# Seven products of quarters for the memory queries and a convolution input, and sums of x in two steps

## What is computed

```python
proj = x @ w_in                                        # (576, 1024) @ (1024, 8192)
cb, cc, ch, rq, rk, rv, rg, mq, gl = split(proj)       # mq: memory queries, 4 x 128 columns; cc: 4 x 128
conv_y = short_conv(cc * ch, ...)                      # cc is the convolution's second input
mk, mv = mem @ w_mem_kv                                # memory keys and values, just before mq
...
hdn = square(relu(x @ w_up))                           # four groups g of 1024 columns
x = layer_norm(alpha * x + hdn @ w_down)
```

## Time and profile before

| | us |
|---|---|
| median of 3 runs | 2177.59 |
| lowest, highest | 2177.37, 2181.48 |
| the profiled execution: its own time | 2177.93 |
| the profiled execution: its span | 2176.1 |
| TensorE busy in that span | 2133.9 |
| GpSimd busy | 1324.7 |
| VectorE busy | 1083.9 |
| ScalarE busy | 508.9 |

### The profile page before, as it was taken

The page is one execution under the profiler, slowest core; times in us unless marked ns, Lnnn a source line. Parts: engine busy times, 40 slices in busy tenths (PEclk is TensorE's granted clock), DMA queues, the critical chain, the costliest instruction groups (busy, mean ns, idle before and its releaser), DMA issues.

```text
span 2176.1 us, 39024 instructions
## 1 busy us (share of the span) xinstructions
PE 2133.9 (98%) x16116; PEld 2088.5 (96%) x16116; DVE 1083.9 (50%) x1713; ACT 508.9 (23%) x909; POOL 1324.7 (61%) x1545
## 2 busy tenths in 40 slices
PE   8999999999999999999999999999999999999997
PEld 8998999999998999999999989999999989999997
DVE  7156300533278863525791572006424798625257
ACT  3121011041013242414141210210410231414132
POOL 6644557645684938375866446676456758475574
PEclk9999999999999999999999999999999999999999
DMA  5324424234221323222324143332342213122321
GB/s 184 112 58 160 128 81 136 73 107 165 83 97 59 97 74 102 78 78 79 96 63 123 59 158 114 114 119 69 115 166 89 87 59 97 60 96 78 98 88 54
DMA packets 199928, 215.23 MB, mean 99 GB/s; under 512 B 5216, under 2 KB 192608, under 8 KB 199776
## 3 DMA queue, kind: packets, MB, share of 16 engines
q1 hardware_dynamic: 170304, 172.84, 25.5%
q10 hardware_dynamic: 29472, 40.20, 5.5%
HBM read 199.06 MB, written 13.97 MB: 98 GB/s over the span
## 4 chain that ended last, share of the span: by engine, by line
PE 91%; DVE 8%; ACT 1%; issue 0%; DMA 0%; ACTq 0%; DVEq 0%
PE gp L524 50%; PE gp L1038 12%; PE gp L540 7%; PE gp L550 7%; PE qb L630 6%; PE gp L693 4%; PE gp L867 1%; PE gp L879 1%; PE qb L661 1%; PE gp L688 1%; DVE r L2048 1%; DVE x_sum L2065 1%; DVE r L1939 1%; DVE dacc L1895 0%; DVE qb L1936 0%; DVE sqacc L1924 0%
## 5 line engine op out<-in xcount | busy, mean ns | idle before, releaser
L439 POOL TENSOR_TENSOR w_lo<-stage,w_hi 128x256 fp32r<-128x256 f32 x1072 | 870.8, 843 | 52.5 <-ACT w_hi L1250 30.0
L436 POOL TENSOR_SCALAR w_hi<-stage 128x1024 fp32r<-128x1024 f32 (+1 forms) x268 | 287.4, 1073 | 567.4 <-PE gp L524 258.1
L524 PE MATMUL gp<-b_hi,w_hi 128*128 128x288 f32 x1408 | 305.9, 299 | 7.0 <-DVE r L2060 7.0
L524 PE MATMUL gp<-x_hi,w_hi 128*128 128x288 f32 x1408 | 304.0, 298 | 0.0
L524 PE MATMUL gp<-b_hi,w_lo 128*128 128x288 f32 x1408 | 302.5, 297 | 0.0
L524 PE MATMUL gp<-b_lo,w_hi 128*128 128x288 f32 x1408 | 302.3, 296 | 0.0
L524 PE MATMUL gp<-x_lo,w_hi 128*128 128x288 f32 x1408 | 301.2, 295 | 0.0
L524 PE MATMUL gp<-x_hi,w_lo 128*128 128x288 f32 x1408 | 301.1, 295 | 0.0
L524 PEld LDWEIGHTS gp<-b_hi,w_hi 128*128 128x128 f32 x1408 | 228.1, 190 | 11.3 <-issue 11.0
L524 PEld LDWEIGHTS gp<-x_hi,w_hi 128*128 128x128 f32 x1408 | 226.9, 189 | 2.9 <-issue 2.6
L524 PEld LDWEIGHTS gp<-b_hi,w_lo 128*128 128x128 f32 x1408 | 227.9, 190 | 0.0
(11 more groups left out here) (275 smaller groups left out, 4371.5 us busy)
## 6 DMA issues: line engine op xcount, KB each, us to landing
stage<-in_w_in SPq DMA_DIRECT2D x62, 1024.0 KB, 5.8
stage<-in_w_up SPq DMA_DIRECT2D x32, 1024.0 KB, 5.4
stage<-in_w_down SPq DMA_DIRECT2D x32, 1024.0 KB, 5.0
stage<-in_w_ret_out SPq DMA_DIRECT2D x8, 1024.0 KB, 5.3
stage<-in_w_mem_kv SPq DMA_DIRECT2D x8, 1024.0 KB, 4.9
stage<-in_w_out SPq DMA_DIRECT2D x8, 1024.0 KB, 4.9
s_in_c<-in_ret_state ACTq DMA_DIRECT2D x8, 512.0 KB, 4.6
out_ret_sample<-s_in_c ACTq DMA_DIRECT2D x8, 512.0 KB, 3.4
```

Of the source, the lines that this page charges most:

```text
L436: nc.gpsimd.tensor_scalar(hi, raw, 1.0, 1.0, ALU.mult, ALU.mult).then_inc(hi_done, 1)
L439: ins = nc.gpsimd.tensor_tensor(lo[:, k:k + 2, :], raw[:, k:k + 2, :], hi[:, k:k + 2, :].bitcast(F32), ALU.subtract)
L524: last = mm(gp[:, 2 * (i % 2) + half, 0:HALF], w[:, i % 4, k * P:(k + 1) * P], x(k, half), start=(n == 0), stop=(n == 3 * nk - 1))
```

## The change

- The eight tiles of `T_MQ` and `T_CC` are made as a group 0 of `seven_products`: four pairs in each layer. Their x sums are made by VectorE, ScalarE and VectorE into new names `q_hi` and `q_lo` (in the memory of `b_hi` and `b_lo`), with `tmp` in the place of `x_sum`. Pair and semaphore counts are renumbered, and the functions that stood in the MLP part are now defined earlier.
- VectorE runs all four `row_sums(0, k)`, `row_sums_low(0, k)`, then the weight sums of the first pair, behind its last step of the retention branch (`T_RO` + 15). ScalarE's `sums_high(0, i)` (that makes `q_hi`) stands behind `weights_high(T_KV + 4 + i)`, before the copy of key tile i + 1.
- `mq` and `cc` are written by VectorE's `quarter_out`, no more by ScalarE.
- In group 0 of the MLP, `row_sums(1, k)` stands behind down tile 2k and `row_sums_low(1, k)` behind down tile 2k + 1; ScalarE's `sums_high(1, k)` are spread among `raw_to_bank` and `seven_high` of group 1.
- TensorE waits for all x sums before the third product of the first pair (the second wait of this kind stood ahead of group 1).

```diff
@@ gpsimd
-            with pool.Fori(0, (T_AM - T_MQ) // RING) as it:
-                split_four(l, it * RING + T_MQ)
+            seven_splits(l, 0)
+            split_four(l, T_CH, behind=(0, pair_no(l, 0, 3)))
+            split_four(l, T_CB)
@@ tensor
-            with pe.Fori(0, 4) as j:
+            for p in range(4):
+                seven_products(0, p)
+            with pe.Fori(2, 4) as j:
                 for i in range(4):
                     product(l, j * 4 + T_MQ + i, j * 2 + (T_MQ + i) // 2, i, *X)
...
+                if p == 0 and g < 2:
+                    pe.wait_ge(s_split, l * 8 + 4 * g + 4)
                 pe.wait_ge(t_split, 4 * q + 1)
                 one(2, c, rows_sum(0), True)
@@ scalar
+            def sums_high(g, k):
+                act.wait_ge(s_made, l * 8 + 4 * g + k + 1)
+                if k:
+                    act.wait_ge(s_split, l * 8 + 4 * g + k)
+                act_fn(sums_of(g)[0][:, :, k, :], s_raw[:, :, :], ACT.Copy).then_inc(s_high, 1)
...
                 weights_high(T_KV + 4 + i)
+                sums_high(0, i)
+            act.wait_ge(b_ready, l * 9 + 9)
+            raw_to_bank(0, 0)
             for i in (0, 2):
                 tile_is_done(act, l, T_KV + 5 + i)
...
+                for n in ((0, 1, 2, 3) if i == 0 else (4, 5, 6)):
+                    seven_high(0, 0, n)
...
-            for t0, buf, s in ((T_MQ, mq, mq_ready), (T_CC, cc, cc_in)):
-                for i in range(4):
-                    tile_is_done(act, l, t0 + i)
-                    act_fn(halves(buf[:, i, :]), pair(i % 2), ACT.Copy).then_inc(s, 1)
+            seven_aside(0)
@@ vector
+            for k in range(4):
+                row_sums(0, k)
+                row_sums_low(0, k)
+            weight_sum(0, 0, 1)
+            sum_low(0, 0, 1)
...
+            seven_aside(0, queries_or_gates)
@@ vector, down tiles of group 0
-                        if g == 0 and m < 4:
-                            row_sums(m)
-                            row_sums_low(m)
+                        if g == 0:
+                            (row_sums_low if m % 2 else row_sums)(1, m // 2)
```

More of the change, by code:

```diff
@@ L322, in pair_no, with hidden_no, first_tile, sums_of @@
     def pair_no(l, g, p):
+        return (l * 4 + g) * 4 + p
+    def hidden_no(l, g, p):
         return (l * 3 + g - 1) * 4 + p
+    def first_tile(g):
+        return T_FF + 16 * g if g else T_MQ
+    def sums_of(g):
+        return (s_hi, s_lo) if g else (q_hi, q_lo)
+    def out_of_pair(g, p):
+        return (relu, relu_odd)[p % 2] if g else (mq, cc)[p // 2][:, 2 * (p % 2):2 * (p % 2) + 2, :]
     def seven_slot(w, n):
@@ L1022, in _ @@
             closing_four(l, T_WO + 4, 0, *M)
[L1024 to L1050, removed]
-                pe.wait_ge(part_in, 4 * q + 1)
-                one(3, a, rows_sum(1), False)
-                pe.wait_ge(raw_split, 3 * q + 3)
-                pe.wait_ge(part_in, 4 * q + 2)
-                one(4, c, rows_sum(3), False)
-                pe.wait_ge(t_split, 4 * q + 3)
-                pe.wait_ge(part_in, 4 * q + 3)
-                one(5, a, rows_sum(2), False)
-                pe.wait_ge(t_split, 4 * q + 4)
-                pe.wait_ge(quarter_made, 4 * q + 1)
-                one(6, b, rows_of(1, 1), True)
-                pe.sem_inc(tile_done, 2)
             def mlp(g, first=False, last=False):
@@ L1474, in _ @@
                 relu_tile(0, i)
-            for k in range(4):
-                act.wait_ge(s_made, l * 4 + k + 1)
-                if k:
-                    act.wait_ge(s_split, l * 4 + k)
-                act_fn(s_hi[:, :, k, :], s_raw[:, :, :], ACT.Copy).then_inc(s_high, 1)
-            def raw_to_bank(g, p):
-                q = pair_no(l, g, p)
-                pair_landed(act, l, g, p)
-                if q:
-                    act.wait_ge(t_split, 4 * q - 1)
-                act_fn(t_sum(2), quarter(p, 0, 1), ACT.Copy).then_inc(b12_in, 1)
@@ L1512, in _ @@
                     seven_high(g, 0, n)
[L1513 to L1536 removed]
+                seven_aside(g)
@@ new lines, in seven_aside @@
+            def seven_aside(g, done):
+                for p in range(4):
+                    more = p < 3
+                    if more:
+                        weight_sum(g, p + 1, 1)
+                    quarter_out(g, p, 0)
+                    if more:
+                        sum_low(g, p + 1, 1)
+                        weight_sum(g, p + 1, 2)
+                        weight_sum(g, p + 1, 3)
+                        sum_low(g, p + 1, 2)
+                        weight_sum(g, p + 1, 4)
+                    quarter_out(g, p, 1)
+                    quarter_out(g, p, 2)
+                    done(p, 1)
+                    if more:
+                        sum_low(g, p + 1, 3)
+                    quarter_out(g, p, 3)
+                    done(p, 0)
+                    if more:
+                        sum_low(g, p + 1, 4)
```

307 lines of the change are left out of this document (174 added, 133 removed).

## The result

| | median | runs | lowest to highest |
|---|---|---|---|
| before | 2178.11 us | 22 | 2176.26 to 2181.48 |
| changed | 2182.53 us | 22 | 2179.77 to 2185.47 |

The ratio is 1.0018, with a 95% interval of 1.0012 to 1.0024. The change makes the kernel slower by 4.4 us. The two ranges overlap by 1.7 us, but the interval of the ratio excludes 1, so the difference is clear of noise; it stands at the edge of the 0.2% that the prediction set as its bound. The forecast was 2182.5 us. The profiled execution took 2183.93 us, its span is 2182.1 us. One execution of the kernel before, 6053 us long at a granted clock of 0.34, fell among those timed beside the first experiments and is left out of every median and ratio.

The account below looks back on a forecast made before the run. TensorE, busy in 98% of the span, was taken as the bound. For both layers 2177.93 - 13.1 (matmuls) - 10.6 (MLP sums) + 28.6 (later first product) = 2182.8 us; median 2182.5, range 2178 to 2186.

Parts of the forecast that it names:

- Fewer matmuls: Group 0: four pairs by seven products, 44.65 us, replace eight tiles, 51.19; saves 6.54 us a layer, 13.1 in both.
- The sums of the MLP in two steps: Down tiles of group 0: TensorE's wait for x sums goes away, saving 5.3 us a layer, 10.6 in both.
- upper end: Down tiles of group 0: saving of 11.9 us if TensorE also keeps the pace of the first tiles.
- The instants of the ring: Key and value tiles: waits among VectorE, ScalarE and GpSimd, followed in five steps, delay the first product 14.3 us a layer.
- What is hidden: Group 0 pairs: weight sums, quarter results, raw splits and removed copies cost 0; 0 to +4 for the first pair.
- The new wait on ScalarE is the larger one: Key and value tiles: ScalarE's wait for sums blocks key copies and value weights; first product 14.3 us later a layer.
- VectorE alone would be late: Before the third product, due at 341.4: VectorE's sums, free to start at 315.9, run at 0.52 speed beside a split.
- The Trainium skill's rule of the exclusive lock: Sums beside GpSimd splits: VectorE and GpSimd block each other for whole instructions; six sums would need 6.1 us, not 5.24.
- The rival that the sums are early enough: Key and value tiles: sums of a k take 3.3 to 4.2 us, delay 4.4 to 10 a layer; faster, 12%.
- The rival of turns: Key and value tiles: port pair alternates, sums of 6.1 us and longer splits, 17.5 us a layer, 2189 us; 10%.
- The rival that the first pairs starve: First pairs of group 0: TensorE waits behind ScalarE's queue, up to 4 us a layer, 2188 us; 8%.
- The rival that the two steps don't help: Down tiles of group 0: 5 to 10 us of wait stay, 2188 to 2193 us; 5%.

Follow-up runs that it names:

- the first experiments: Each part by itself against the kernel before: only the MLP sums in two steps, 2168.38 us; only mq and cc by seven products, 2194.0 us.
- where the sums are early: Changed kernel with raw x sums of all four k made during the retention gates into their own buffer, q_lo behind the last value split: 2156.08 us.
- The two-by-two table: Changed kernel with ScalarE's roundings moved later, 2185.4 us; plus a second raw-sum buffer, 2176.4; plus GpSimd making one of four low-weight pieces, 2176.5; plus both, 2163.6.
- the kernel without sums: Changed kernel with VectorE's six x sums of each k in group 0 replaced by one short instruction; waits, roundings and products kept: 2164.82 us.
- the kernel with two buffers: Changed kernel with ScalarE's roundings behind its key copies and value weights, and a second buffer for the raw sums: 2176.41 us.

## Why the prediction was right

- **The number**, 2182.5 forecast and 2182.53 measured: the mechanism is the one that was forecast, but the agreement to a tenth is luck. The terms missed by 0.9 and 0.5 us in opposite directions, the median of the kernel before rose by 0.5 us with more runs, and the traced sum (+5.3) stands 0.9 above the difference of the medians. More than 0.2% slower, which had 58%, isn't what the ratio shows: 0.18%, with an interval that reaches over the bound.
- **Fewer matmuls**, -13.1: right; 44.63 against 51.19 us in both layers.
- **The sums of the MLP in two steps**, -10.6: 9.7 in the trace. In layer 0 only 4.5 us came back and not 5.3, because the five tiles ahead of the first wait took 31.21 us before, where five tiles at the usual pace take 32.0. That pace, which the prediction named as an upper end, was not there in the changed kernel. It isn't tied to the change: in other kernels of the study it is there in one layer and not in the other, as the 74.88 us above show. Alone the part gave 10.6 us between medians.
- **The instants of the ring**: `q_hi` at 321.8, 329.9, 337.8 and 345.7 predicted, 320.93, 329.13, 336.95 and 344.71 measured; V0 at 331.5 and 330.76, V1 at 344.8 and 343.93, first product at 352.5 and 351.76. All are 0.7 to 1.0 us early, of which 0.6 is the earlier start of the layer's last retention tile. The split of 4.15 us and the sums of 5.2 to 5.3 us carried over from the down tiles, where they were read, to the key tiles (4.23 and 5.1 to 5.6). The low clock behind the second gap cost 2.1 us, with 1.8 taken.
- **What is hidden**, 0: right. No wait stands between the first product and the last of group 0. The two stores of ScalarE cost nothing in the changed kernel; in the kernels with less delay they do show (1.1 us ahead of the fourth product where the sums are early).
- **"The new wait on ScalarE is the larger one"**: right as a description of who blocked whom, and wrong as a statement of what it costs. With that wait gone the time did not fall. The prediction's own step of costs for VectorE alone ("VectorE alone would be late") was broken off at the rate of the sums beside a split and not carried on to the third product; it would have shown that this limit stands right behind the other.
- **The Trainium skill's rule of the exclusive lock**, set aside for the measured 5.24 us: for the sums the row was the better guide (5.1 to 5.6 a k, not 6.1). For one long `q_lo` against one piece the rule describes what the trace shows.
- The rival that the sums are early enough needed cycles under 7 us; they were 7.8 and 8.2. The rival of turns needed 8.7. The rival that the first pairs starve fell with the 44.63 us; its price of 2188 doesn't fit its own "up to 4 us a layer", which would be 2190.5 (2182.5 + 8). The rival that the two steps don't help fell with the 76.79 us.

What stays open is how the 14 us a layer divide between VectorE, GpSimd and ScalarE. The two-by-two table gives 9 us in both layers to each of two reliefs and leaves 8 to 10 us to neither. It can't tell a plain sum from reliefs that strengthen each other. It wasn't tried whether ScalarE's two stores behind the first kept part would take away the last 1 us a layer.

## What to carry to other kernels

When a change puts work beside other work, add up what every engine has to do between the last instant that it may begin and the first at which it is awaited, at the rate that the engines have beside each other; if the sum is longer than the room, altering the order only moves the wait. Look then for a stretch further ahead where the engine waits for TensorE and its inputs already exist: the same instructions, no faster, cost nothing there. And run the parts of a change one by one: here one gave 0.5% and the other took 0.7%, and together they looked like nothing.

## What the runs showed of the hardware

- A GpSimd subtraction of 128x256 elements that meets a VectorE subtraction of 1152 elements a partition took 1.85 us in place of 0.71. Beside shorter ones of VectorE (288 elements, 0.46 us alone and 0.88 beside a split) it took 1.04 to 1.07.
- The low clock follows gaps that look alike only sometimes. In the kernel without sums both layers have gaps of 1.51 and some 2.05 us ahead of the two value tiles. At full clock a value tile takes 5.76 us; the second tile then took 7.51 us in layer 0 and 6.02 in layer 1. The chain of that kernel:

```profile
336.77 7.51 PE gp L897 x48
...
1410.46 6.02 PE gp L897 x48
```

  Windows over these tiles show a granted clock of 0.79 in the first and 1.00 in the second:

```profile
336.00:344.00 8.00, 7.23 (x48) 7.23 (x49) 3.98 (x6) 2.89 (x6) 3.53 (x6) 0.79 0.44 132
1410.00:1416.00 6.00, 5.54 (x46) 5.54 (x47) 3.28 (x5) 1.87 (x4) 3.20 (x5) 1.00 0.58 176
```

  A single gap of 1.06 us brought no fall. In the kernel with two buffers the second value tile stood behind gaps of 3.66 and 3.65 us in the two layers and then took 1.5 us more than 5.76 in the one and 3.0 in the other:

```profile
338.21 7.26 PE gp L900 x48
...
1413.42 8.75 PE gp L900 x48
```

  So a gap's price here is its length and between nothing and some 3 us more, and I would not give it more closely.
